# The output of carried states: four turned products straight into the TensorE accumulation

## The chip, the cores and the metric

One core of a Trainium2 chip runs the whole kernel in one launch. The metric is the device time of that launch in microseconds; the figure for a kernel is the median of its runs. TensorE does matmuls into PSUM, VectorE (DVE), ScalarE (ACT) and GpSimd (POOL) do elementwise work, SyncE (SP) issues most loads, and every engine executes its own instructions in program order and waits on semaphores.

## What is computed

The reference is one layer of a hybrid backbone, run for two groups of 128 tokens (a context pass, g = 0, and a denoising step, g = 1) with d_model 1024, in f32:

```
h  = rmsnorm(x) * (1 + scale) + shift            # scale, shift from silu(c) @ w_mod
u, c_q, c_kv, k_rope = split(h @ w_in)
ssm  = s5_mixer(u)                               # 32 groups x 64 complex states, forward and backward scan
attn = latent attention(c_q, c_kv, k_rope)       # 8 heads
x += g1 * ([ssm, attn] @ w_out)
x += g2 * peer(norm2(x))                         # 8 heads, top 16 of 128 x 128 experts, rows of 1024 + 1024
```

The part that the change touches is the state-space mixer. For every direction it computes h[t] = A h[t-1] + B u[t] with complex diagonal A, and adds to the output y[t] = Re(C h[t]) = C_re h_re - C_im h_im, summed over both directions. It also returns the last (or, backward, first) state h as new_ssm.

## The kernel before

**Units and chunks.** The 512 channels are cut in four units u = 0..3, each with 8 rows a = 4 d + j (direction d, four pairs j of channel groups); partitions hold two halves e of 64 states. Time is cut in 32 chunks of 4 steps (STEP), so that the scan runs over chunks, on 33 values (SL) with the initial state in front. What a chunk's own inputs give to its outputs is y_local (L581), a matmul with a small Toeplitz matrix. What the state at the chunk's start gives is y_carried (L592), a matmul with ypow, the powers of A times C for four steps.

**The states of a unit.** A complex scan with a rotating A is made real: the inputs are turned back by the chunk's angle (s5_products, L1547, VectorE; sums by s5_sums, L1350, GpSimd), scanned with a real decay (s5_scans, L1557, VectorE), and the results g_re, g_im are turned forward again. The turn gives four products in the four slots of the unit's work buffer, view(u, 0) to view(u, 3): VectorE's s5_turns (L1567) writes slot 0 = cos g_re and slot 2 = - sin g_im, and counts qd_ready; GpSimd's s5_turns (L1364) turns slots 1 and 3 in place into sin g_re and cos g_im, and counts qp_ready. Then GpSimd adds slot 2 to slot 0 (real part) and slot 3 to slot 1 (imaginary part), each 128 x 528, L1371, and counts sum_ready. s5_last (L1373) copies the last state out of slots 0 and 1 into hlast, 128 x 8 for each part, and counts last_ready.

**TensorE's order** is written out by hand. Between the state-space steps stand those of the projections, the modulation (quad_step L460, pair_step L477, each on a 1 MB page of weights) and attention. Around the change it is

```
toeplitz(0); toeplitz(1)         # L532
latents_turned(0)                # L503
y_local(0); y_carried(0)         # L589, L601
quad_step 4, 5                   # L466
latents(1); y_spread(0); attention_queries(0); attention_keys(0, 0)
y_local(1); y_carried(1); quad_step 6, 7; latents_turned(1); y_spread(1); heads_turned(0)
y_local(2); y_carried(2); attention_scores(0); y_spread(2)
y_local(3); y_carried(3); pair_step a 0, a 1; y_spread(3); probs_turned(0) ...
```

y_carried(u) adds onto what y_local(u) began in bank 4 + u % 2 and counts y_ready. ScalarE copies that bank to SBUF (y_evac, L1083, copy at L1085); y_spread (L606) puts it in order of time, waiting for that copy; VectorE adds the skip term (L1575).

**ScalarE's order** has y_evac(2), then attention_exp(0) (L1055), the scaling of the probabilities (L1216), then y_evac(3). latents_scaled (L1000, L1005) waits for a root that GpSimd makes (inverse_root, L1325, L1329) between unit 2 and unit 3.

**Who waits for the states.** y_carried(u) waits for sum_ready 2u + 2. SP waits for y_ready 4 and last_ready 8 (L415, L416) before it loads the second half of w_out, the keys and further weights, since their pages lie over the work buffers. ScalarE waits for last_ready 8 at L1221.

**Experts.** Query projections and scores (TensorE, ScalarE) lead to a top-16 search on VectorE (find, number), whose indices GpSimd's gathers wait for (L1406): 256 gathers, each of 128 rows of 8 KB, into a ring of pages. VectorE takes dot products with the row (L1738), ScalarE makes a diagonal of the weight (L1143), TensorE accumulates (L789) and frees the row for a later gather. GpSimd's gathers stand in its order behind everything of the state-space part.

Of the kernel before, what the change touches and what calls it, by code (L numbers as in the profile page):

```python
# [13 lines left out]
ALU = mybir.AluOpType  # L14
# [14 lines left out]
CHUNKS = P // STEP  # L29
# [93 lines left out]
def layer(nc, x_prompt, x_sample, consts_in, powers_in, w_mod01, w_mod2, b_mod, w_in_u, w_in_qkv, bmat, cmat,  # L123
# [5 lines left out]
    with ExitStack() as ctx:  # L129
# [3 lines left out]
        def sem(name):  # L133
            return ctx.enter_context(nc.semaphore(name))
# [153 lines left out]
        def row_of(pick):  # L288
# [18 lines left out]
        rad4_ready, dec_ready, bu_ready, bu_used, prod_ready, v_ready, g_ready, qd_ready, qp_ready, last_ready = (  # L307
            sem(n) for n in ("rad4_ready", "dec_ready", "bu_ready", "bu_used", "prod_ready", "v_ready", "g_ready",
                             "qd_ready", "qp_ready", "last_ready"))
        sum_ready, out_used, cols2_ready, rootd_ready = (sem(n) for n in ("sum_ready", "out_used", "cols2_ready", "rootd_ready"))  # L310
        y_ready, ysb_ready, ysh_ready, y_read, yg_ready, ygh_ready, ssm_ready = (
            sem(n) for n in ("y_ready", "ysb_ready", "ysh_ready", "y_read", "yg_ready", "ygh_ready", "ssm_ready"))
        q_ready, k_ready, nb_ready, exp_ready, rr_ready, probs_ready = (
# [33 lines left out]
        def view(u, k):  # L347
            return work[u][:, k, :].rearrange("p (a g n) -> p a g n", a=8, g=G)

        def table(u, s, lo, hi):  # L350
            return tabs[:, s, 8 * u:8 * u + 8, lo:hi].unsqueeze(2).to_broadcast([P, 8, G, hi - lo])

        def chunks(ap, d):
            return ap[:, :, ::-1] if d else ap
# [82 lines left out]
        def _(pe):  # L437
# [152 lines left out]
                                  tile_position=(64 * e, 64 * e))  # L590

            def y_carried(u):  # L592
                pe.wait_ge(sum_ready, 2 * u + 2)
                out = psum[:, 4 + u % 2, :]
                for j in range(4):
                    for d in range(2):
                        a = 4 * d + j
                        for r in range(2):
                            for e in range(2):
                                es = slice(64 * e, 64 * e + 64)  # L600
                                mm = pe.matmul(out[es, 64 * j:64 * j + 64], ypow[es, r, 8 * u + a, 1:5, :].rearrange("p k q -> p (k q)"),  # L601
                                               chunks(view(u, r)[es, a, :, 0:CHUNKS], d),
                                               start=False, stop=j == 3 and d == 1 and r == 1, tile_position=(64 * e, 64 * e))
                mm.then_inc(y_ready, 1)

            def y_spread(u):  # L606
# [232 lines left out]
            latents_turned(0)  # L839
            y_local(0)  # L840
            y_carried(0)
            quad_step(1, 4)
            quad_step(1, 5)
# [3 lines left out]
            attention_keys(0, 0)  # L847
            y_local(1)
            y_carried(1)
            quad_step(1, 6)  # L850
            quad_step(1, 7)
            latents_turned(1)
            y_spread(1)
            heads_turned(0)
            y_local(2)
            y_carried(2)
            attention_scores(0)
            y_spread(2)
# [449 lines left out]
        def _(pool):  # L1308
            n = [0]
# [29 lines left out]
            for e in range(2):  # L1339
                es = slice(64 * e, 64 * e + 64)  # L1340
# [23 lines left out]
            def s5_turns(u):  # L1364
                for r, (k, tab) in enumerate(((1, 1), (3, 0))):
                    pool.wait_ge(qd_ready, 2 * u + r + 1)
                    pool.tensor_tensor(view(u, k), view(u, k), table(u, tab, 0, SL), ALU.mult).then_inc(qp_ready, 1)

                for r in range(2):
                    pool.wait_ge(qp_ready, 2 * u + 2)  # L1370
                    pool.tensor_tensor(view(u, r), view(u, r), view(u, 2 + r), ALU.add).then_inc(sum_ready, 1)  # L1371

            def s5_last(u):  # L1373
                pool.wait_ge(sum_ready, 2 * u + 2)
                hl = hlast.rearrange("p (d r c j) -> p d r c j", d=2, r=2, c=NC)
                for r in range(2):
                    pool.tensor_copy(hl[:, :, r, u, :], view(u, r)[:, :, 0, CHUNKS].rearrange("p (d j) -> p d j", d=2)).then_inc(last_ready, 1)

            def available(page_):
                if page_ == 6:  # L1380
# [29 lines left out]
            for u in range(NC):  # L1410
                if u + 1 < NC:
                    s5_sums(u + 1)
                if u == 3:
                    inverse_root(rstd_a[:, 0:2], ms_a[:, 0:2], [(0, 1, QR), (1, 2, KVR)], sqa_ready, 2, rstda_ready)
                s5_turns(u)
                s5_last(u)
# [531 lines left out]
```

## Time and profile before

| what | us |
|---|---|
| median of 3 runs | 924.32 |
| lowest, highest | 923.16, 925.59 |
| profiled execution, its own time | 921.98 |
| its span | 920.2 |
| PE busy | 761.9 (83%), 4033 instructions |
| DVE busy | 562.1 (61%) |
| ACT busy | 341.9 (37%) |
| POOL busy | 354.8 (39%) |
| mean DMA rate | 350 GB/s, 322.00 MB |

The profile is of one execution; its own time is the span and the little that lies around it. Busy time is a share over the whole span, and stages differ, so the slices and windows below say more than the sums. The trace shows an f32 matmul as two pairs of a weight load (PEld) and a matmul (PE). "Idle before" is the engine's idle time just ahead of a group, with what ended it; "issue" means that nothing in the profile explains it.

### The profile page before, as it was taken

The page shows a single profiled execution, that of the slowest core. Times are in us where ns is not written, and L with a number is a line of the kernel's source. Part 1 is how long each engine was busy: PE and PEld are TensorE (multiplying, and loading weights), DVE is VectorE, ACT ScalarE, POOL GpSimd, SP SyncE. Part 2 cuts the span into 40 slices and gives each one's busy share as a digit, 9 for nine tenths or more (in the row PEclk, how much of TensorE's full clock was granted, in tenths as well). Part 3 has the DMA queues.
Part 4 walks back from the last instruction along what each step waited for, and adds up shares of the span by engine and source line. Part 5 has one row for each costly group of instructions (what it writes and reads, how often), then busy time and mean ns, then how long its engine had stood idle before and what let it go on. Part 6 is the DMA issues. An engine that isn't in the chain of part 4 may idle for free. (4 is left out here: it accounts for less than half of the span.)

```text
span 920.2 us, 11502 instructions
## 1 busy us (share of the span) xinstructions
PE 761.9 (83%) x4033; PEld 388.1 (42%) x4033; DVE 562.1 (61%) x1225; ACT 341.9 (37%) x1008; POOL 354.8 (39%) x334
## 2 busy tenths in 40 slices
PE   3898898997879799999898887985896697598875
PEld 0576665465443265556454222431332232142221
DVE  7977311173847855864775459558846954875444
ACT  3412236024543453443252325433432443353331
POOL 3328600002323435353434514542664364275420
PEclk8899899999889899999999998997999799799998
DMA  9842466316679999999998999999999999999993
GB/s 369 363 176 89 181 237 255 137 48 275 228 265 414 416 420 417 421 422 421 421 420 311 424 421 422 420 422 422 421 422 422 422 421 423 422 420 422 422 421 129
DMA packets 45953, 322.00 MB, mean 350 GB/s; under 512 B 5372, under 2 KB 5948, under 8 KB 7880
## 3 DMA queue, kind: packets, MB, share of 16 engines
q0 software_dynamic: 36864, 268.45, 70.8%
q1 hardware_dynamic: 8664, 52.63, 14.7%
q8 instruction: 32, 0.52, 0.2%
q10 hardware_dynamic: 368, 0.18, 0.1%
q14 instruction: 25, 0.20, 0.1%
HBM read 320.02 MB, written 1.23 MB: 349 GB/s over the span
## 5 line engine op out<-in xcount | busy, mean ns | idle before, releaser
L789 PE MATMUL psum<-mem 128*128 128x512 f32 x1024 | 488.8, 623 | 109.2 <-ACT mem L1143 108.2
L1738 DVE CUSTOM_DVE_ANT_0 mem<-mem,h 128x1024 f32<-128x1024 f32 x256 | 309.0, 1225 | 227.4 <-DMA mem<-uv_table,small 222.8
L1406 POOL DMA_INDIRECT mem<-uv_table,small x256 | 291.5, 1139 | 396.0 <-PE psum L789 309.3
L789 PEld LDWEIGHTS psum<-mem 128*128 128x128 f32 x1024 | 191.7, 197 | 392.5 <-issue 198.6
L1136 ACT ACTIVATE small<-small 128x1 f32<-128x1 f32 x256 | 51.9, 203 | 374.8 <-DVE small L1738 366.2
L1143 ACT ACTIVATE mem<-consts,small 128x128 f32<-128x128 f32 x256 | 102.9, 402 | 8.4
L1139 ACT ACTIVATE small<-small 128x1 f32<-128x1 f32 x256 | 75.4, 295 | 24.8 <-ACT small L1136 1.1
L745 PEld LDWEIGHTS psum<-hT,mem 128*128 128x128 f32 x512 | 59.3, 192 | 7.8 <-issue 7.8
L745 PE MATMUL psum<-hT,mem 128*128 128x128 f32 x512 | 59.8, 275 | 2.3 <-ACT mem L1061 2.3
L1328 POOL TENSOR_SCALAR small<-small 128x1 f32<-128x1 f32 (+1 forms) x9 | 2.9, 318 | 127.4 <-DVE small L1638 65.1
L466 PE MATMUL psum<-mem,scol 128*32 128x512 f32 x128 | 21.2, 766 | 17.0 <-DMA mem<-w_mod 17.0
L715 PE MATMUL psum<-mem,hT 128*128 128x512 f32 x64 | 28.6, 594 | 0.0
L1577 DVE SCALAR_TENSOR_TENSOR yb<-h,consts,psum 128x256 f32<-128x256 f32 x4 | 1.9, 480 | 41.6 <-PE psum L611 41.6
L1694 DVE FIND_INDEX8 mem<-mem 128x8 uint32<-128x128 f32 (+1 forms) x64 | 21.9, 352 | 0.0
L966 ACT COPY late<-psum 128x512 f32<-128x512 f32 (+3 forms) x37 | 19.4, 570 | 6.2 <-PE psum L652 2.4
L966 ACT COPY mem<-psum 128x512 f32<-128x512 f32 (+2 forms) x20 | 10.6, 539 | 29.2 <-PE psum L532 16.2
L1738 DVE DVE_READ_ACCUMULATOR2_ANT small<- 128x1 f32 x256 | 21.2, 83 | 0.0
L1691 DVE MAX8 mem<-mem 128x8 f32<-128x128 f32 (+1 forms) x64 | 20.0, 352 | 1.1
L715 PEld LDWEIGHTS psum<-mem,hT 128*128 128x128 f32 x64 | 11.8, 190 | 14.2 <-issue 14.2
L1552 DVE TENSOR_TENSOR mem<-psum,mem 128x512 f32<-128x512 f32 x16 | 9.9, 684 | 11.7 <-PE psum L576 11.7
L522 PE MATMUL psum<-hT,mem 128*128 128x256 f32 x64 | 14.6, 383 | 2.0 <-ACT hT L978 2.0
L532 PE MATMUL psum<-h,consts 128*32 128x64 f32 x512 | 13.2, 271 | 3.2 <-issue 3.2
(212 smaller groups left out, 647.8 us busy)
## 6 DMA issues: line engine op xcount, KB each, us to landing
mem<-w_mod SPq DMA_DIRECT2D x24, 1024.0 KB, 9.0
mem<-w_query SPq DMA_DIRECT2D x8, 1024.0 KB, 8.2
mem<-w_out SPq DMA_DIRECT2D x4, 1024.0 KB, 5.0
mem<-uv_table,small POOLq DMA_INDIRECT x256, 23.5
mem<-w_in_u SPq DMA_DIRECT2D x2, 1024.0 KB, 14.3
mem<-w_in_qkv SPq DMA_DIRECT2D x2, 1008.0 KB, 10.0
mem<-w_uq SPq DMA_DIRECT2D x2, 576.0 KB, 8.3
mem<-w_ukv SPq DMA_DIRECT2D x1, 1024.0 KB, 6.0
```

Source lines behind the costliest of these rows:

```text
L466: mm = pe.matmul(out[32 * j:32 * j + 32, :], scol[:, k, :], w[:, j, :], start=k == 0, stop=k == KD - 1, tile_position=(0, 32 * j))
L715: mm = pe.matmul(out, mixT[:, k, P * g:P * g + P], weight(f"out{half}.{k // 4}", 512, 4)[:, k % 4, :], start=first and i == 0, stop=last a ...
L745: mm = pe.matmul(bank(name)[:, P * i:P * i + P], weight(m, 512, 4)[:, k % 4, P * i:P * i + P], hT[:, k, P * g:P * g + P], start=k == 0, st ...
L789: mm = pe.matmul(bank(f"acc_{g}_{half}"), diag[:, pick % DEEP, :], row_of(pick)[:, D + 512 * half:D + 512 * half + 512], start=first and k ...
L966: empties(act.copy(dst, src), name)
L1136: act.activation(gel[:, cut_], dots[:, cut_], ACT.Gelu_apprx_tanh).then_inc(gel_ready, 1)
L1139: act.activation(wts[:, cut_], gel[:, cut_], ACT.Copy, scale=gate[:, pick:pick + 1]).then_inc(wts_ready, 1)
L1143: act.activation(diag[:, slot, :], ident, ACT.Copy, scale=wts[:, cut_]).then_inc(diag_ready, 1)
L1406: pool.indirect_dma_start(row_of(pick), None, uv_table, bass.IndirectOffsetOnAxis(ap=idx[:, pick:pick + 1], axis=0)).then_inc(row_landed[R ...
L1691: last = dve.max(out_v[:, r, first_:first_ + 8], row)
L1694: last = dve.max_index(out_i[:, r, first_:first_ + 8], out_v[:, r, first_:first_ + 8], row)
L1738: dve.tensor_tensor_reduce(out=row[:, 0:D], in0=row[:, 0:D], in1=h[:, it // NB, :], scale=1.0, scalar=0.0, op0=ALU.mult, op1=ALU.add, accu ...
```

## The change

GpSimd's two additions for each unit are gone, and sum_ready with them. y_carried(u) waits for all turned products of the unit and runs over four (weight, slot) pairs in place of two: the real weight with slots 0 and 2, the imaginary weight with slots 1 and 3. Its matmuls for each unit go from 32 to 64. s5_last adds the two slots of each part where it copied one.

```
             def y_carried(u):
-                pe.wait_ge(sum_ready, 2 * u + 2)
+                pe.wait_ge(qd_ready, 2 * u + 2)
+                pe.wait_ge(qp_ready, 2 * u + 2)
                 out = psum[:, 4 + u % 2, :]
                 for j in range(4):
                     for d in range(2):
                         a = 4 * d + j
-                        for r in range(2):
+                        for k, (r, b) in enumerate(((0, 0), (0, 2), (1, 1), (1, 3))):
                             for e in range(2):
                                 es = slice(64 * e, 64 * e + 64)
                                 mm = pe.matmul(out[es, 64 * j:64 * j + 64], ypow[es, r, 8 * u + a, 1:5, :].rearrange("p k q -> p (k q)"),
-                                               chunks(view(u, r)[es, a, :, 0:CHUNKS], d),
-                                               start=False, stop=j == 3 and d == 1 and r == 1, tile_position=(64 * e, 64 * e))
+                                               chunks(view(u, b)[es, a, :, 0:CHUNKS], d),
+                                               start=False, stop=j == 3 and d == 1 and k == 3, tile_position=(64 * e, 64 * e))
                 mm.then_inc(y_ready, 1)
...
                     pool.tensor_tensor(view(u, k), view(u, k), table(u, tab, 0, SL), ALU.mult).then_inc(qp_ready, 1)
 
-                for r in range(2):
-                    pool.wait_ge(qp_ready, 2 * u + 2)
-                    pool.tensor_tensor(view(u, r), view(u, r), view(u, 2 + r), ALU.add).then_inc(sum_ready, 1)
 
             def s5_last(u):
-                pool.wait_ge(sum_ready, 2 * u + 2)
+                pool.wait_ge(qp_ready, 2 * u + 2)
                 hl = hlast.rearrange("p (d r c j) -> p d r c j", d=2, r=2, c=NC)
-                for r in range(2):
-                    pool.tensor_copy(hl[:, :, r, u, :], view(u, r)[:, :, 0, CHUNKS].rearrange("p (d j) -> p d j", d=2)).then_inc(last_ready, 1)
+                for r, (a_, b_) in enumerate(((0, 2), (1, 3))):
+                    pool.tensor_tensor(hl[:, :, r, u, :], view(u, a_)[:, :, 0, CHUNKS].rearrange("p (d j) -> p d j", d=2),
+                                       view(u, b_)[:, :, 0, CHUNKS].rearrange("p (d j) -> p d j", d=2), ALU.add).then_inc(last_ready, 1)
```

## Rows read from the trace of the kernel before

**Rows 1.** The page's 40 slices of 23 us: busy tenths, DMA tenths, DMA rate.

```profile
PE   3898898997879799999898887985896697598875
DMA  9842466316679999999998999999999999999993
GB/s 369 363 176 89 181 237 255 137 48 275 228 265 414 416 420 417 421 422 421 421 420 311 424 421 422 420 422 422 421 422 422 422 421 423 422 420 422 422 421 129
```

**Rows 2.** Windows: stretch, length, busy (PE, PEld, DVE, ACT, POOL), PE clock, DMA share, GB/s.

```profile
107.40:143.00 35.60, 35.27 (x471) 23.84 (x467) 4.43 (x12) 11.25 (x28) 1.77 (x4) 1.00 0.56 212
```

**Rows 3.** The page: the gathers' DMA queue, and two of the costliest groups.

```profile
q0 software_dynamic: 36864, 268.45, 70.8%
...
L1738 DVE CUSTOM_DVE_ANT_0 mem<-mem,h 128x1024 f32<-128x1024 f32 x256 | 309.0, 1225 | 227.4 <-DMA mem<-uv_table,small 222.8
L1406 POOL DMA_INDIRECT mem<-uv_table,small x256 | 291.5, 1139 | 396.0 <-PE psum L789 309.3
```

**Rows 4.** Timeline of PE, DVE, POOL: start, length, instruction, idle before and releaser.

```profile
197.56 0.61 PE L769 MATMUL psum<-mem,yb 128*128 128x128 f32 x4
...
198.69 0.49 DVE L1691 MAX8 mem<-late 128x8 f32<-128x128 f32 x2 [1.56 <-ACTq L1124]
...
208.83 1.21 POOL L1406 DMA_INDIRECT mem<-uv_table,small  x1 [20.87 <-DVEq L1721]
```

**Rows 5.** Timeline of PE around y_carried of units 0, 1 and 3.

```profile
104.82 2.67 PE L601 MATMUL psum<-mem 64*64 64x64 f32 x64
107.42 1.92 PE L466 MATMUL psum<-mem,scol 128*32 128x512 f32 x16
...
127.97 2.03 PE L601 MATMUL psum<-mem 64*64 64x64 f32 x64
129.93 1.92 PE L466 MATMUL psum<-mem,scol 128*32 128x512 f32 x16
...
138.03 2.05 PE L676 MATMUL psum<-late 96*128 96x128 f32 x16
...
141.11 2.03 PE L601 MATMUL psum<-mem 64*64 64x64 f32 x64
143.07 3.63 PE L484 MATMUL psum<-mem,scol 128*32 128x512 f32 x16
```

**Rows 6.** Timeline of PE behind unit 3, with its waits.

```profile
148.74 0.65 PE L611 MATMUL psum<-h,consts 128*32 128x64 f32 x32 [2.04 <-ACT h L1085]
...
155.04 3.84 PE L705 MATMUL psum<-yb,mem 128*128 128x128 f32 x32 [1.88 <-ACT yb L1224]
```

**Rows 7.** POOL: group of the adds (busy, mean ns), timeline of the latents' root and last adds.

```profile
L1371 POOL TENSOR_TENSOR mem<-mem 128x528 f32<-128x528 f32 x8 | 11.6, 1472 | 0.3
...
100.67 0.71 POOL L1329 TENSOR_TENSOR small<-small,half_neg 128x2 f32<-128x2 f32 x1
...
103.83 2.57 POOL L1371 TENSOR_TENSOR mem<-mem 128x528 f32<-128x528 f32 x2
```

**Rows 8.** Windows around unit 0 (columns as in rows 2).

```profile
102.70:104.80 2.10, 2.10 (x22) 1.77 (x23) 0.00 (x0) 2.06 (x7) 2.02 (x2) 0.50 0.00 0
...
106.30:106.80 0.50, 0.50 (x24) 0.50 (x20) 0.00 (x0) 0.00 (x0) 0.41 (x3) 1.00 0.00 0
```

**Rows 9.** Timeline of ACT: group 0's latents, and the copy for unit 3.

```profile
101.42 0.58 ACT L1005 ACTIVATE late<-psum,small 128x384 f32<-128x384 f32 x1 [7.84 <-POOL small L1329]
...
148.34 0.35 ACT L1085 COPY h<-psum 128x256 f32<-128x256 f32 x1
```

**Rows 10.** Timeline of PE: stops inside groups of small matmuls.

```profile
79.34 1.13 PE L551 MATMUL psum<-mem,yb 128*32 128x64 f32 x87 [1.48 <-issue]
...
82.79 0.92 PE L576 MATMUL psum<-mem 64*64 64x64 f32 x24 [0.99 <-issue]
...
100.53 2.19 PE L532 MATMUL psum<-h,consts 128*32 128x64 f32 x73 [3.17 <-issue]
```

**Rows 11.** SP's own queue: the loads that wait for unit 3.

```profile
143.18 1.71 SPq L383 DMA_DIRECT2D mem<-w_out  x2
```

More of the change, by code:

```diff
@@ L309, in layer @@
                              "qd_ready", "qp_ready", "last_ready"))
-        sum_ready, out_used, cols2_ready, rootd_ready = (sem(n) for n in ("sum_ready", "out_used", "cols2_ready", "rootd_ready"))
+        out_used, cols2_ready, rootd_ready = (sem(n) for n in ("out_used", "cols2_ready", "rootd_ready"))
         y_ready, ysb_ready, ysh_ready, y_read, yg_ready, ygh_ready, ssm_ready = (
```

## The prediction

> **What bounds the kernel now.** I read the page's slices first. They show two regimes. From the thirteenth slice (276 us) to the end the DMA digits stand at 9 and the bytes run at about 420 GB/s; ahead of that the DMA has holes and the PE digits are at 8 and 9 [rows 1]. The windows say the same: in 107.4 to 143 us the DMA share is 0.56 while TensorE is busy 35.27 of 35.60 us [rows 2]. The late regime is the gather of expert rows: 268.45 MB over 256 gathers is 1.049 MB each, at 421 GB/s 2.49 us each [rows 1, 3], and VectorE's 227.4 us of idle time there are put down to these rows [rows 3]. Its length is bytes over bandwidth; when it starts is what the early part decides. So the question for an edit in the early part is whether it moves the first gather.
>
> Back from there: the first gather goes out at 208.83 us, released by VectorE's list of indices; VectorE began that search at 198.69, released by ScalarE's copy of the scores that TensorE had made at 197.56 [rows 4]. TensorE executes in program order, and from 104.8 us on it is a nearly gapless stream: y_local, y_carried (L601) and the next step stand end to end, with no idle in front of any of the L601 groups [rows 5]. The longest waits of TensorE between there and the first gather are 2.04 us at 148.74 (for ScalarE's copy L1085) and 1.88 us at 155.04 [rows 6]. They are waits for work that TensorE itself feeds, so they move with it, except where the feeding step lies ahead of what is added.
>
> GpSimd, which the change relieves, has the eight adds (L1371, 11.6 us together) done by 106.4 us, and TensorE asks for unit 3's sums at 141.11 [rows 5, 7]. Nobody waits for the adds here.
>
> **The change, part by part.**
> Matmuls. y_carried(u) has 32 matmuls, which the trace shows as 64 pairs of weight load and matmul (two for each f32 matmul). After it has 64, or 128 pairs: the sum of the turned products is made in the accumulation. The 64 pairs take 1.96 us at full clock: from 127.97 to the next group at 129.93, and from 141.11 to 143.07; unit 2 repeats it up to 138.03 [rows 5]. That is 30.6 ns a pair. Unit 0 took 2.60 us (104.82 to 107.42 [rows 5]): the granted clock was 0.50, the 1.2 GHz level, after TensorE had stood still for 3.17 us, and was back at 1.00 by 106.3 [rows 8]. What is added to unit 0 comes behind its first 64 pairs, when the clock is back, so it too costs 1.96 us. With the clock still low it would be up to twice that, 3.9.
> A page puts the price lower. The Trainium skill, "TensorE: Matmul & The Clock Gate", section on the back-to-back issue gap, has a floor of about 25 ns from start to start for matmuls of up to 64 columns. At that price 64 pairs are an estimated 1.6 us, and three units 4.8 instead of 5.9.
> The trace has 30.6 ns for this very instruction, and that is taken.
>
> What of it lies on the path. Units 0, 1 and 2: TensorE is busy before and after each, so each adds its whole 1.96 us; 3 x 1.96 = 5.9. Unit 3: behind its y_carried stand two modulation steps (L484) and then the wait of 2.04 us until 148.74 [rows 5, 6]. It is set by ScalarE: the exponentials of group 0, their scaling, then the copy for unit 3 at 148.34 to 148.69 [rows 9]. That chain starts from attention_scores(0) at 138.03, ahead of y_carried(3), so it moves by 5.9 and not by the fourth 1.96, which goes into the wait: 2.04 - 1.96 leaves 0.08 us. Unit 3 costs nothing; with that cover gone it would cost 1.96. Nor does ScalarE come to wait for it: the last matmul of unit 3 will end near 143.07 + 4 x 1.96 = 150.9, and ScalarE gets to its copy at 148.34 + 5.9 = 154.2.
>
> GpSimd. Out go 11.6 us of adds. s5_last becomes two adds on 8 columns in place of two copies on 8: price 0, and the whole of GpSimd's part could grow by several us before unit 1's products are late for 127.97. One thing behind the adds in GpSimd's order has a waiter: the root for group 0's latents (L1329, 100.67), for which ScalarE's L1005 waits until 101.42 [rows 7, 9]. It comes some 3 us earlier, by unit 2's two adds of 1472 ns. But TensorE still had 2.19 us of L532 to do from 100.53 [rows 10], up to 102.7, and then went straight on; an earlier latent gives it nothing. I take 0 and the bounds 0 and -0.5, the time from ScalarE's latents (101.42 + 1.0) to the end of L532, and a little more.
>
> Waits. TensorE waits for qd_ready and qp_ready instead of sum_ready. The first two come before the third did, and no new instruction is queued behind a longer wait; 0. SP's queue: six loads and the two rows of constants that wait for unit 3's y_ready go out from 143.18 on [rows 11]; now from 151. The first two (w_out, 2 MB) are 5 us at 420 GB/s, so down by 157, and their first user stands behind the gate projection, at 155.04 + 5.9 = 160.9 [rows 6]. Hidden, and the others are needed later still; were they late, the cost would be some of the 7.8 us less this margin of 4.
>
> Instruction supply. Before 100 us TensorE stops in the middle of groups of small matmuls with "issue" as the reason: 1.48 us at 79.34, 0.99 at 82.79, 3.17 at 100.53. Between the first two lie 87 pairs and the 40 of the next group of 64 (24 follow the stop), 127 in all, and 3.45 us [rows 10]. I read that as instructions arriving in blocks of some 127 pairs, at 3.5 us a block while the DMA is quiet, slower while it is full. 127 pairs of y_carried take 3.9 us, and with wider neighbours each block in the changed stretch should last 5 us or more. I take 0; the bounds are 0 and 3.2, the longest stop.
> The Trainium skill, "Runtime: NRT & Kernel Launch", section on instruction fetch mechanics, calls the crossing of such a block "mostly hidden"; by that the term is 0 outright. The three stops disagree with it for dense small matmuls, which is why the term stays in the range.
>
> Sum: 3 x 1.96 = **+5.9 us**. The profiled execution took 921.98 us (span 920.2, 1.8 around it) and would take 927.9. It lies 2.3 under the median of the runs, 924.32; against that median the forecast is **930.2 us**, +0.64%.
>
> **Rivals.**
> Absorbed before the end (not slower, 924.3 us). Mechanism: the gathers between 208 and 276 us run at 228 to 275 GB/s [rows 1], so a later start is caught up there. It decides if at least 3 us of the 5.9 is caught up. For it: those holes. Against: the holes come from gathers that wait for TensorE to free rows (most of GpSimd's idle 396 us [rows 3]), and TensorE for ScalarE's diagonals, which is one loop that starts later as a whole. Chance 0.10.
> Instruction stops in the doubled groups (931 to 933.4). For: the three stops. Against: from 104 to 143 us the same groups had none. One stop more costs 1 to 3.2 us. Chance 0.15.
> The fourth unit is exposed (932.2). The margin is 0.08 us; with TensorE later by a little, up to 1.96 more. Chance 0.10.
> The added pairs cost less than the mean of those before, as their weights are loaded twice in a row: at the 4.8 us above, or any price down to 25 ns, 929.1. Chance 0.05.
> The change doing less than it says isn't likely: the four products are written out in the loop. The forecast itself has 0.60.
>
> **How the numbers follow.** About 0.3% (2.8 us) is what a measurement can tell from no change. All cases but the first lie over that bound, so slower is 0.87, the runs' own scatter (923.16 to 925.59, some 1.2 us to each side) taken off; the absorbed case gives same 0.10, and 0.03 is left to faster, for a gain of GpSimd's that I don't see. The range: 930.2 less the scatter, GpSimd's 0.5 and the cheaper pairs gives the lower end, 927.3; the upper takes in the exposed fourth unit or a stop, with scatter, 934.0. The absorbed case stays outside.
>
> **What the changed profile would show.** L601 with 512 pairs, 128 a unit, 3.92 us a unit at clock 1.00 and about 4.6 for unit 0, no idle in front of them. L1371 gone. The wait for L1085 shrunk from 2.04 to about 0.1 us. The first gather at 214.7 in place of 208.83, and the DMA full from about 282. ScalarE's L1005 some 3 us earlier, without effect. The prediction is wrong if the first gather moves by 6 us and the end doesn't, if L601 runs at another price than 30.6 ns, or if "issue" stops stand inside L601.

## The result, and the profile after

The changed kernel takes 929.96 us, median of 5 runs (928.43 to 930.71), against 924.32 us (923.16 to 926.23, 5 runs): a ratio of 1.0053 with an interval of 1.0034 to 1.0072. It is slower by about half a per cent. The forecast was 930.2 us. The profiled execution took 928.43 us, with a span of 926.6.

The page's slices of the changed kernel, to be read against [rows 1]:

```profile
PE   3898898998779699989989787984897698498875
DMA  9852454526579999999997999999999999999993
GB/s 372 355 188 75 162 215 185 200 91 240 186 288 385 421 409 418 420 422 420 422 419 312 423 421 421 420 422 420 422 421 422 422 420 423 422 420 422 422 421 133
```

The late part has not changed: the same 421 GB/s from the fourteenth slice to the end. What has moved is its start. The thirteenth slice (278 to 301 us) stands at 385 GB/s where it stood at 414.

The groups that answer to [rows 3], and the queue that brings instructions (32 packets before), from the page:

```profile
q0 software_dynamic: 36864, 268.45, 70.3%
...
q8 instruction: 34, 0.56, 0.2%
...
L1737 DVE CUSTOM_DVE_ANT_0 mem<-mem,h 128x1024 f32<-128x1024 f32 x256 | 308.9, 1225 | 227.5 <-DMA mem<-uv_table,small 221.6
L1405 POOL DMA_INDIRECT mem<-uv_table,small x256 | 294.3, 1150 | 393.0 <-PE psum L790 307.7
```

VectorE's wait for rows (227.5 us) and GpSimd's (393.0) are what they were to within 3 us. So nothing behind the first gather pays or gains.

TensorE's timeline around the four L602 groups (y_carried, L601 before); it answers to [rows 5] and [rows 6]:

```profile
104.59 4.59 PE L602 MATMUL psum<-mem 64*64 64x64 f32 x128
109.12 1.92 PE L466 MATMUL psum<-mem,scol 128*32 128x512 f32 x16
...
129.67 3.90 PE L602 MATMUL psum<-mem 64*64 64x64 f32 x128
133.50 1.92 PE L466 MATMUL psum<-mem,scol 128*32 128x512 f32 x16
...
139.62 2.32 PE L602 MATMUL psum<-mem 64*64 64x64 f32 x73
142.84 1.84 PE L602 MATMUL psum<-mem 64*64 64x64 f32 x55 [0.90 <-issue]
144.62 2.05 PE L677 MATMUL psum<-late 96*128 96x128 f32 x16
...
147.70 3.90 PE L602 MATMUL psum<-mem 64*64 64x64 f32 x128
151.53 3.63 PE L484 MATMUL psum<-mem,scol 128*32 128x512 f32 x16
155.33 0.65 PE L612 MATMUL psum<-h,consts 128*32 128x64 f32 x32 [0.18 <-ACT h L1086]
```

The sum can be read off. Unit 0 lasts 4.53 us from its start to the next group's start, where it lasted 2.60: +1.93. Unit 1: 3.83 for 1.96, +1.87. Unit 2: 5.00 for 1.97, +3.03, with a stop in it. Unit 3 lasts 1.87 us more too, but the wait for ScalarE's copy behind it has gone from 2.04 to 0.18 us: 0. TensorE came to unit 0 0.23 us earlier, as it had ended its early stop (82.79 us in [rows 10]) 0.23 us earlier. 1.93 + 1.87 + 3.03 - 0.23 = 6.60 us, and this is just what the first gather shows: 215.43 us for 208.83.

```profile
215.43 1.22 POOL L1405 DMA_INDIRECT mem<-uv_table,small  x1 [20.88 <-DVEq L1720]
```

From the first gather to the end of the span it was 711.4 us and is 711.2. The whole 6.4 us by which the span has grown lie ahead of the first gather.

### The profile page after: what moved, and what is told of

It is laid out like the page before. It is cut to its first block and busy times, and to the rows that moved or that the text cites. A ratio compares the mean times of both kernels' runs of the same rounds, so it can differ in the third digit from the quotient of the medians.

```text
span 926.6 us, 12010 instructions
## 1 busy us (share of the span) xinstructions
PE 770.3 (83%) x4289; PEld 397.3 (43%) x4289; DVE 560.7 (61%) x1225; ACT 342.2 (37%) x1008; POOL 345.2 (37%) x326
## 5 line engine op out<-in xcount | busy, mean ns | idle before, releaser
L1737 DVE CUSTOM_DVE_ANT_0 mem<-mem,h 128x1024 f32<-128x1024 f32 x256 | 308.9, 1225 | 227.5 <-DMA mem<-uv_table,small 221.6
L1405 POOL DMA_INDIRECT mem<-uv_table,small x256 | 294.3, 1150 | 393.0 <-PE psum L790 307.7
L602 PE MATMUL psum<-mem 64*64 64x64 f32 x512 | 16.6, 223 | 0.9 <-issue 0.9
L602 PEld LDWEIGHTS psum<-mem 64*64 64x64 f32 x512 | 16.1, 140 | 1.0 <-issue 1.0
```

The costliest lines, as they stand in the source:

```text
L1405: pool.indirect_dma_start(row_of(pick), None, uv_table, bass.IndirectOffsetOnAxis(ap=idx[:, pick:pick + 1], axis=0)).then_inc(row_landed[R ...
L1737: dve.tensor_tensor_reduce(out=row[:, 0:D], in0=row[:, 0:D], in1=h[:, it // NB, :], scale=1.0, scalar=0.0, op0=ALU.mult, op1=ALU.add, accu ...
```

## The experiments

Two readings are used for each run. One is the ratio to the kernel before on the same chip. The other is from the trace, and leaves out the part behind the first gather, which varies by some 6 us between executions (710.8 to 716.8): the **stretch** from the end of the last early stop (the row of L576 with 24 pairs, at 82.79 in [rows 10]) to the first gather. It was 208.83 - 82.79 = 126.04 us before, and is 215.43 - 82.56 = 132.87 in the changed kernel.

The stretch comes from one execution, and TensorE's granted clock is not alike in all of them. A second profile of the changed kernel gave 133.96 us, 1.1 more. Falls of the clock can be read off in two places. From y_spread(3) (L611) to the end of TensorE's next wait it takes 6.30 us before (148.74 to 155.04), and 7.9 to 8.0 where the clock fell. From there to the first gather it takes 53.8 us before, and 55.4 where it fell. Each fall is 1.6 to 1.7 us, and it is named where a stretch has one. It can't be put down to an edit: of the changed kernel's two profiles the second has one, in the second place, and the first has none. Without it the second is at 132.35 us.

My theory: the price is TensorE's time for the added pairs in units 0 to 2, unit 3's is hidden, GpSimd's relief is worth nothing where the kernel stands, and a stop of the instruction supply (TensorE out of instructions to execute, "issue" in the rows) was added. Rivals: every unit pays; the shorter GpSimd queue gains; the stop belongs to something else.

### GpSimd's adds out, matmuls not doubled

```
-                        for k, (r, b) in enumerate(((0, 0), (0, 2), (1, 1), (1, 3))):
+                        for k, (r, b) in enumerate(((0, 0), (1, 1))):
```

> The changed kernel with y_carried over slots 0 and 1 alone (two products, 64 pairs a unit, as before): GpSimd's adds and their waits are gone, the matmuls are not doubled. The carried part leaves out slots 2 and 3. Theory (the whole price is TensorE's time for the added pairs; GpSimd's relief is worth nothing): as the kernel before, 924.3 us, within 0 to -0.5; the wait for L1085's copy is back at about 2.0 us; the first gather at 208.3 to 208.9. Rival (the shorter GpSimd queue itself gains, and the price of the pairs is larger than it looks): 3 us or more below the kernel before, and ScalarE's latents, 4 us earlier, show as an earlier y_local(0).

Measured: ratio 1.0006 (0.9982 to 1.0031). The stretch is 208.31 - 82.54 = 125.77 us, 0.3 under that of before. By the ratio the relief of GpSimd alone gives nothing clear of some 2 us; the trace has to say more, and TensorE's timeline has things in it that were not expected:

```profile
100.29 1.22 PE L532 MATMUL psum<-h,consts 128*32 128x64 f32 x73 [3.18 <-issue]
...
102.66 1.15 PE L602 MATMUL psum<-mem 64*64 64x64 f32 x33
104.23 1.15 PE L602 MATMUL psum<-mem 64*64 64x64 f32 x31 [0.42 <-issue]
...
146.62 0.87 PE L612 MATMUL psum<-h,consts 128*32 128x64 f32 x32 [2.04 <-ACT h L1086]
154.54 3.84 PE L706 MATMUL psum<-yb,mem 128*128 128x128 f32 x32 [1.88 <-ACT yb L1225]
```

First, a stop inside unit 0, after 73 + 5 (L503) + 16 (L589) + 33 = 127 pairs: the count that separated the stops in [rows 10]. Second, from the wait of 2.04 us to the next wait it takes 7.92 us where it took 6.30 [rows 6]. The windows say why; the first line is the kernel before from 148.70, the second this run from 146.60 (columns as in rows 2):

```profile
148.70:155.00 6.30, 4.42 (x60) 2.85 (x60) 0.48 (x1) 4.39 (x7) 0.00 (x0) 1.00 1.00 367
```

```profile
146.60:154.50 7.90, 6.04 (x60) 4.11 (x60) 0.48 (x1) 4.49 (x7) 0.00 (x0) 0.78 0.95 386
```

The same 60 matmuls, with the granted clock at 0.78 in place of 1.00: behind the wait it was down at its 1.2 GHz level for a while. It costs 1.6 us here.

It hides a gain of 1.9 us. Unit 0 starts 20.12 us behind the early stop (102.66 - 82.54) where it started 22.03 behind it (104.82 - 82.79). That gain is the clock's too and not GpSimd's: toeplitz resumes after the same 17.7 us in both, and the 94 pairs from there to unit 0 take 2.37 us at a granted clock of 1.00 where they took 4.29 at 0.50. The changed kernel, which has no adds either, took 4.28. TensorE waits for nothing of GpSimd's in either timeline. So the relief is worth 0 here, and the price sits in the doubled matmuls.

### One unit, and three units

```
+FOUR = (3,)        # second run: (0, 1, 2)
...
+                parts = ((0, 0), (0, 2), (1, 1), (1, 3)) if u in FOUR else ((0, 0), (1, 1))
...
-                for r in range(2):
+                for r in range(0 if u in FOUR else 2):
                     pool.wait_ge(qp_ready, 2 * u + 2)
                     pool.tensor_tensor(view(u, r), view(u, r), view(u, 2 + r), ALU.add).then_inc(sum_ready, 1)
```

> The kernel before with the four products on TensorE for unit 3 alone; units 0 to 2 keep GpSimd's adds. Theory (unit 3's pairs go into TensorE's wait for ScalarE's copy): time as before, 924.3 us, within 0.5; L601's last group 3.83 us in place of 1.96, the wait behind it 0.2 in place of 2.04. Rival (every unit pays): +1.9 us, 926.2.

> The kernel before with the four products on TensorE for units 0, 1 and 2; unit 3 keeps GpSimd's adds. Theory: the whole price of the change, +5.7 to +6.6 us, 930 to 931; the wait behind unit 3 back at about 2.0 us; an issue stop of about 0.9 us inside unit 2 at the same place, since the instruction stream up to there is the changed kernel's. Rival (each unit's share is a quarter): +4.4 us, 928.7.

Measured: unit 3 alone 1.0009 (0.9985 to 1.0033); units 0 to 2 1.0077 (1.0053 to 1.01). The stretches are 126.06 and 133.15 us, so 0.0 and +7.1; the first holds no fall of the clock, the second one. TensorE's timeline with unit 3 alone changed:

```profile
142.67 3.90 PE L607 MATMUL psum<-mem 64*64 64x64 f32 x128
...
150.30 0.65 PE L617 MATMUL psum<-h,consts 128*32 128x64 f32 x32 [0.17 <-ACT h L1091]
156.60 3.84 PE L711 MATMUL psum<-yb,mem 128*128 128x128 f32 x32 [1.88 <-ACT yb L1230]
```

128 pairs at no cost, since the wait shrinks by as much. With units 0 to 2 changed:

```profile
136.52 2.32 PE L607 MATMUL psum<-mem 64*64 64x64 f32 x73
139.45 1.84 PE L607 MATMUL psum<-mem 64*64 64x64 f32 x55 [0.61 <-issue]
...
144.31 2.03 PE L607 MATMUL psum<-mem 64*64 64x64 f32 x64
...
151.93 0.65 PE L617 MATMUL psum<-h,consts 128*32 128x64 f32 x32 [2.03 <-ACT h L1091]
159.91 3.84 PE L711 MATMUL psum<-yb,mem 128*128 128x128 f32 x32 [1.88 <-ACT yb L1230]
```

The stop after the same 73 pairs of unit 2 is there, and the wait of 2.03 us is back. 7.98 us from there to the next wait: the clock fell once more (0.79 over 151.9 to 159.9). Without that fall the stretch is +5.4 us. Another 1.1 us was saved at unit 0, which came 0.4 us earlier behind the early stop and ran at full clock (3.83 us for 4.53); with the changed kernel's clock there the price would be 6.5 us, an estimate, by its stop of 0.61 us in place of 0.90 a little under the 6.8 of all four units (132.87 - 126.04). So "a quarter for each unit" is out: unit 3 alone costs 0.0, where it would have cost 1.5.

### The pairs twice over

```
-                        for k, (r, b) in enumerate(((0, 0), (0, 2), (1, 1), (1, 3))):
+                        for k, (r, b) in enumerate(((0, 0), (0, 2), (1, 1), (1, 3)) * 2):
```

> The changed kernel with y_carried's four products made twice over (256 pairs a unit), so that the carried part is doubled. Theory: 128 more pairs a unit at 29.9 ns are 3.83 us, now exposed in all four units but for 0.2: 4 x 3.83 - 0.2 = +15.1 over the changed kernel, so about 945 us, plus issue stops of 0 to 4 us where the DMA is busy (near units 0 and 2); 945 to 949. Rival (the early part has slack that takes in what is added, the gathers catch up): less than 940.

Measured: 945.43 us, ratio 1.0247 (1.0209 to 1.0284). The stretch is 227.11 - 81.12 = 145.99 us, +13.1 over the changed kernel; unit 0 ran at full clock from its start here (7.56 us up to 110.03), which is 0.8 less than the changed kernel's 4.53 + 3.83, and TensorE came to it 0.7 us earlier behind the early stop. That is most of what is missing from the 15.1 expected.

```profile
102.47 7.63 PE L602 MATMUL psum<-mem 64*64 64x64 f32 x256
110.03 1.92 PE L466 MATMUL psum<-mem,scol 128*32 128x512 f32 x16
...
144.27 2.32 PE L602 MATMUL psum<-mem 64*64 64x64 f32 x73
147.46 5.58 PE L602 MATMUL psum<-mem 64*64 64x64 f32 x183 [0.88 <-issue]
```

256 pairs in 7.56 us are 29.5 ns a pair: the price is linear. There is no slack ahead of the gathers that takes in what is added, and the absorbed case is out at 15 us too. The stop stands in unit 2 after 73 pairs again, although 256 pairs were put in ahead of it: 256 is two blocks of 127 and 2. The page's instruction queue counts the same blocks:

```profile
q8 instruction: 38, 0.62, 0.3%
```

It is 32 packets for the kernel before, 34 with 256 more pairs, 38 here with 512 more again: one packet for every 128 pairs.

### Is it the supply of instructions?

Two experiments move what the DMA does while small matmuls run. One holds two loads back in the changed kernel; the other puts toeplitz ahead of the quad steps that release four loads, in the kernel before.

```
             for n in range(ORDER["mod1.0"], ORDER["out1.0"]):
+                if PAGES[n][0] == "mod2a.0":
+                    sp.wait_ge(y_ready, 3)
                 load(PAGES[n][0])
```

> The changed kernel with SP waiting for unit 2's y_ready before it loads mod2a.0 and mod2a.1, which in the changed kernel start at 134.6 us and run beside unit 2. Theory (the stop of 0.90 us inside unit 2, 634 = 5 x 127 pairs behind the stop at 100.3, is a block that comes late since the DMA is full): no stop in unit 2, attention_scores(0) 0.9 us earlier; the loads start near 143.8 and take 6 to 8 us, and their user L484 at 150.6 may wait up to 1 us, partly inside the wait behind it: time 0 to -0.9 us against the changed kernel's +5.6. Rival (the stop belongs to the place in the stream alone): the 0.9 us stop stays.

Measured: ratio 1.0042 (1.0024 to 1.006), stretch 211.34 - 80.08 = 131.26 us, 1.6 under the changed kernel's, where 0 to 0.9 were expected. Unit 2 has no stop, and attention's first matmul follows it at once:

```profile
136.31 3.90 PE L604 MATMUL psum<-mem 64*64 64x64 f32 x128
```

The windows before and in unit 2, first of the changed kernel, then of this run:

```profile
134.60:139.60 5.00, 4.67 (x79) 3.44 (x73) 0.48 (x1) 3.88 (x11) 0.00 (x0) 1.00 0.79 285
139.60:142.00 2.40, 2.34 (x81) 2.20 (x75) 0.00 (x0) 0.34 (x1) 0.00 (x0) 1.00 0.69 280
142.00:142.80 0.80, 0.00 (x0) 0.00 (x0) 0.00 (x0) 0.00 (x0) 0.00 (x0) 1.00 0.05 20
```

```profile
131.00:136.30 5.30, 4.97 (x83) 3.57 (x77) 0.48 (x1) 3.89 (x11) 0.00 (x0) 1.00 0.01 3
136.30:140.20 3.90, 3.90 (x136) 3.83 (x131) 0.00 (x0) 0.33 (x1) 0.00 (x0) 1.00 0.02 4
```

The same instructions in the same place, with a DMA share of 0.69 to 0.79 and of 0.01 to 0.02. The rival, a stop that belongs to the place alone, is out. The count sets the place: 634 pairs behind the stop at 100.3 us, which is 5 x 127 but for one. Of the 1.6 us, the stop with its restart is 1.2 (5.00 us for unit 2 became 3.83) and the clock at unit 0 is 0.7 (3.83 for 4.53); 0.4 were lost at L484, whose page now came late. The second profile of the changed kernel has unit 0 at full clock as well (3.83) and still stops for 0.89 us in unit 2, so unit 0's clock is not what took the stop away.

This run alone does not show that the DMA's load causes the stop. At the same place, with the loads where the changed kernel has them, the stop was 0.90, 0.89, 0.88, 0.61 and 0.34 us in five runs, and in a sixth, the changed kernel with two moves that comes below, there was none (0.07 us at most), though the DMA share over that block, 133.66 to 138.80 us, was 0.87:

```profile
136.49 3.97 PE L602 MATMUL psum<-mem 64*64 64x64 f32 x128
```

The better evidence is the time from one block's start to the next where TensorE did stop in between: 3.45 and 3.65 us at a DMA share of 0.03 and 0.15 (79.34 to 82.79 and 75.69 to 79.34 in the kernel before), some 5.1 us at 0.94 (up to 100.53), some 5.5 to 6.0 us at 0.74 to 0.81 in unit 2. TensorE's own work in unit 2's block lasts 5.0 to 5.1 us, so a block that takes 5 to 6 us is sometimes late and one of 3.5 us never.

```
-            quad_step(1, 2)
-            quad_step(1, 3)
             pe.wait_ge(bu_used, NC)
             toeplitz(0)
             toeplitz(1)
+            quad_step(1, 2)
+            quad_step(1, 3)
```

> The kernel before with toeplitz(0) and (1) ahead of quad_step(1, 2) and (1, 3) in TensorE's order; nothing else. In the kernel before the four 1 MB loads that the two quad steps release start at 94.0 us, and the 256 small pairs of toeplitz stop for 3.2 us at issue beside them; TensorE's clock is at 0.50 behind that stop until 106.2. Theory (instructions come in blocks of 127 pairs, in about 3.5 us when the DMA is quiet and 5 when it is full): the stop is still there but shorter, 1.5 to 2 us, and the clock may not fall; -1.5 to -4 us, 920.3 to 922.8. Rival (the stop is a wait for something else in the program, or has nothing to do with the DMA): stop of 3.2 us again, time as before.

Measured: ratio 0.9969 (0.9948 to 0.999), stretch 125.35 us, 0.7 under the kernel before. By the ratio this is within the forecast, by the stretch it is not.

```profile
92.04 2.99 PE L532 MATMUL psum<-h,consts 128*32 128x64 f32 x199
96.18 1.00 PE L532 MATMUL psum<-h,consts 128*32 128x64 f32 x57 [1.15 <-issue]
96.99 1.91 PE L466 MATMUL psum<-mem,scol 128*32 128x512 f32 x16
100.98 1.35 PE L503 MATMUL psum<-consts,late 128*128 128x128 f32 x5 [2.09 <-ACTq L1010]
```

The stop is 1.15 us where it was 3.17 [rows 10]: half confirmed. The block before it, from the 72nd of the 199 pairs (near 93.1 us) to 96.18, took 3.1 us beside a DMA share of 0.02, where some 5.1 us had gone by before. The other half failed. A new wait of 2.09 us stands at the latents' transposes, for ScalarE, which waits for GpSimd's root, which stands behind unit 2's adds; and the clock fell all the same behind it (0.60 over 100.98 to 103.2). GpSimd's adds were off the path only as long as TensorE was held up by something else.

The same move on the changed kernel, which has no adds:

> The changed kernel with toeplitz(0) and (1) ahead of quad_step(1, 2) and (1, 3). Theory: the gain of the same move on the kernel before, -1.5 to -4 us, carries over in full, since both lie on TensorE's gapless stream: 926 to 928.4. In it unit 0's L602 runs at full clock if the clock does not fall, 3.83 in place of 4.53 us.

Measured: ratio 1.0045 (1.002 to 1.0069), stretch 131.14 us, 1.7 under the changed kernel's, and 3.4 under it without a fall of the clock behind the second wait (0.75 over 157.1 to 164). Unit 0 starts at 99.42 us at full clock, with no wait for the latents. But the loads start later by as much, and a quad step now waits for its page:

```profile
99.42 3.90 PE L602 MATMUL psum<-mem 64*64 64x64 f32 x128
...
105.97 1.07 PE L466 MATMUL psum<-mem,scol 128*32 128x512 f32 x8 [1.65 <-DMA mem<-w_mod]
```

So less of the move came through than expected (929.45 us where 926 to 928.4 were forecast): the page and, in the profiled execution, the clock took it. Against the run before this one it also gives the price of the adds in this order: behind the early stop, unit 0 starts after 18.08 us without them and after 21.21 us with them, 3.1 us.

The quad steps between the two toeplitz groups:

> The kernel before with quad_step(1, 2) and (1, 3) between toeplitz(0) and toeplitz(1). Theory of blocks: 1.9 us of wide matmuls between the two groups of 128 pairs give the supply 1.9 us more, but toeplitz(1) now runs beside the four loads: a stop of 1 to 3 us in it, time 0 to -2 us against the kernel before. Rival (the stop depends on the count of small matmuls alone, whatever is between them): 3.2 us, time as before.

Measured: ratio 0.9987 (0.9969 to 1.0005), stretch 125.46 us. No stop is left in toeplitz, where 1 to 3 us were expected, and the wait for the latents is 3.48 us: the stop was traded for it.

### The two moves together

If GpSimd's adds bound the latents once the stop is gone, then either taking them out or going round them must free TensorE. Here the root goes ahead of unit 2's adds, on top of the split order.

```
                     pool.tensor_tensor(view(u, k), view(u, k), table(u, tab, 0, SL), ALU.mult).then_inc(qp_ready, 1)
+                if u == 2:
+                    inverse_root(rstd_a[:, 0:2], ms_a[:, 0:2], [(0, 1, QR), (1, 2, KVR)], sqa_ready, 2, rstda_ready)
```

> The kernel before with quad_step(1, 2) and (1, 3) between the two toeplitz groups, and GpSimd's root for group 0's latents ahead of unit 2's adds in place of behind them. In the split order alone TensorE had no issue stop left, but waited 3.48 us for ScalarE's latents, whose root GpSimd made at 100.5 us, behind unit 2's adds. Theory (GpSimd's adds become the bound there once the stop is gone): the wait at the latents' transposes vanishes, unit 0's L601 starts near 101 in place of 104.8 and at full clock; the loads of the next two weight pages, now issued 2 us later, take back about 1 us; -2.5 to -3.5 us against the kernel before. Rival (the wait has another source): no change against the split order alone, -0.3 us.

> As the run before this, and with the four products on TensorE for unit 3 alone, which fill TensorE's wait of 2.04 us for ScalarE's copy. Theory: the same time within 0.5 us; what the filled wait can save is a fall of the granted clock behind it, which two earlier runs had (0.78 and 0.79 over 8 us, some 1.6 us longer) and which no run with the wait filled had. Rival (unit 3's pairs have a price after all): +1.9 us over the run before this.

> The changed kernel with the same two moves (quad steps between the toeplitz groups; the root between unit 2's products and its last states). Theory: TensorE's start of unit 0 moves forward by the same 3 to 4 us, the price of the pairs (3 x 1.87 us and unit 2's stop) stays: +1.5 to +3.5 us against the kernel before, and 5 to 6.5 us over the first of these runs.

> The changed kernel itself, as a scale for this chip: +5.6 us, ratio 1.0061 (earlier 1.0053, 1.0034 to 1.0072). Theory: first gather 6 to 7 us later than in the kernel before, counted from the stop near 82.7 us; the stretch from the first gather to the end the same within the scatter of 711 to 716 us.

Measured, in this order: 0.9964 (0.9939 to 0.999); with unit 3's four products 0.9941 (0.9912 to 0.997); the changed kernel with both moves 1.005 (1.003 to 1.007); the changed kernel 1.0052 (1.0029 to 1.0075), which repeats the first result (1.0053). TensorE in the first of them:

```profile
98.85 1.09 PE L503 MATMUL psum<-consts,late 128*128 128x128 f32 x5 [1.01 <-ACTq L1010]
...
100.39 1.21 PE L601 MATMUL psum<-mem 64*64 64x64 f32 x34
103.33 1.14 PE L601 MATMUL psum<-mem 64*64 64x64 f32 x30 [1.74 <-issue]
...
145.71 0.65 PE L611 MATMUL psum<-h,consts 128*32 128x64 f32 x32 [2.03 <-ACT h L1085]
153.70 5.47 PE L705 MATMUL psum<-yb,mem 128*128 128x128 f32 x32 [1.88 <-ACT yb L1224]
```

The wait for the latents is 1.01 us for 3.48 (it was to vanish), and unit 0 starts 18.14 us behind the early stop for 21.38 in the split order alone. But TensorE now gets to the next block of instructions sooner than that arrives, and stops for 1.74 us inside unit 0. And in this execution the clock fell behind both waits at the end of the extract (7.99 us between them for 6.30; 5.47 us for the group that took 3.84), so that the stretch is 126.85 us and not shorter than before, while the runs' ratio is. Without the two falls it is 123.55 us, 2.5 under the kernel before. The run with unit 3's products in the wait has the first of these waits at 0.17 us and 6.31 us behind it (147.82 to 154.13); its stretch is 125.45 us with one fall, 123.8 without. The two ratios overlap, so that the filled wait gains something is not shown. That unit 3's pairs cost nothing is: from unit 3's start to the end of the second wait it takes 13.93 us with them, and 13.9 without them once the fall of 1.7 us is taken off. Both ratios lie below 1 by more than their intervals. The second has the lowest median here, 919.63 us, but is not told apart from the first.

In the changed kernel the two moves gave a ratio that can't be told from that of the changed kernel alone, so the 3 to 4 us expected are not shown by it. Its unit 0 stops for 2.04 us in the same place. The stretch is 131.66 us, 130.05 without a fall behind the second wait: 2.3 to 2.8 us under the changed kernel's two profiles, where their falls are taken off too.

## Why the prediction was right

- **What bounds, and what carries to the end.** Right: the first sign named for being wrong, a first gather that moves while the end doesn't, did not show. The first gather moved by 6.60 us and the span by 6.4. The absorbed case was put at 0.10; the run with the pairs twice over shows that 15 us aren't absorbed either.
- **The price of a pair.** 30.6 ns expected, 3.83 us for 128 pairs measured, 29.9 ns. The 1.96 us for 64 had a start in it that isn't paid twice. The floor of about 25 ns that the Trainium skill gives ("TensorE: Matmul & The Clock Gate", back-to-back issue gap) is not reached by this stream of pairs, not even over 256 in a row (29.5). Nor is it a floor for every stream: toeplitz's pairs on 128 x 32 tiles ran at 15.0 ns (199 in 2.99 us).
- **Units 0 to 2 exposed, unit 3 hidden.** Right by the trace and by two runs that separate them: 0.0 and +7.1 us in the stretch (+5.4 without a fall of the clock). The wait left behind unit 3 was to be 0.08 us and is 0.18.
- **Unit 0's clock.** Right: the added 64 pairs ran at full clock, +1.93 us.
- **GpSimd's relief at 0.** Right for this kernel (ratio 1.0006), with ScalarE's latents at 97.52 us in the changed kernel where they were at 101.42. That is 3.9 us earlier and not 3: unit 2's two adds took 3.87 us together, where twice the mean of 1472 ns is 2.9. That it was 0 only because TensorE had its own stop at that time was half said ("TensorE still had 2.19 us of L532 to do") and is the step with the least depth: once that stop is shorter, TensorE waits 2.1 to 3.5 us behind them, and without them unit 0 starts 3.1 us earlier.
- **Instruction supply at 0.** This term was mis-sized, and it is the step that failed: it should have been about 1.2 us. "Issue" stops inside L601 were named as a sign of being wrong, and one stands there. The step said that "each block in the changed stretch should last 5 us or more" and so come in time. The block that ends in unit 2 did last 5.1 us of TensorE's work (from about 136.8 to 141.9), and the next still came 0.9 us late: beside a DMA at 0.69 to 0.79 a block took 6 us. The step had read 3.5 us a block "while the DMA is quiet, slower while it is full", but put no figure on the slower one, though the stop at 100.53 gives it, some 5.1 us. With the slower restart it made unit 2's share 3.03 in place of 1.87. It lies in the term's bounds (0 to 3.2) and was the second rival. The Trainium skill ("Runtime: NRT & Kernel Launch", instruction fetch mechanics) has such crossings "mostly hidden". Here some are, even in small dense matmuls (unit 2 of the run with the loads held), but every trace has three or more that aren't, up to 3.76 us.

That the forecast of 5.9 us lies so near the medians' 5.64 is in part luck. By the trace, counted from the early stop, the change costs 6.8 us: the pairs 5.7 (0.2 less than forecast) and the stop 1.2 (forecast 0). The interval of the ratio is 3.1 to 6.7 us, so the medians can't tell 5.9 from 6.6, and the second comparison, +4.8 us, can't either.

## What to carry to other kernels

Moving an add into TensorE's accumulation isn't free because another engine is rid of it: count the pairs, and ask which of the two engines somebody waits for at that time. The added work is free only inside a wait whose cause lies ahead of it in TensorE's own order, as behind unit 3; there alone the change costs nothing. That it gains anything there is not shown. When a stop is taken away, look for what stands right behind it: here GpSimd's adds, a page of weights and the next block of instructions each took part of a gain back, or all of it. And before a trace of one execution is compared with another, look where the clock fell in each: two falls of 1.6 to 1.7 us hid a gain of 2.5 us here.

## What the runs showed of the hardware

- Streams of small matmuls can stop at every 127th or 128th pair of weight load and matmul, where the next instructions are late. From one block to the next it took 3.1 to 3.7 us beside a nearly idle DMA (share 0.02 to 0.15), and some 5 to 6 us beside a busy one (0.74 to 0.94). 127 pairs at 29.9 ns take 3.8 us. The stops were 0.3 to 3.8 us long, and at one and the same place beside a busy DMA 0 to 0.9 us. The place can be counted ahead, wide matmuls counted as well as small ones.
- A wait of 2 us on TensorE was followed by a fall of the granted clock in three of six executions and not in the others, of the same instructions: 7.9 to 8.0 us for 6.3 (clock 0.78 to 0.79). In the runs that filled that wait there was none behind it, but five of all fourteen profiles had one behind the next wait of 1.88 us, one of the changed kernel's two among them.
- From the first gather to the end, executions differ by up to 6 us (710.8 to 716.8), as much as the effects that were looked for. A stretch cut out of the trace told them apart better than the time of the whole, once the falls of the clock were taken off.
